# Four-K-tile groups in the first projection stage, norm vectors requested ahead of the rows of x, and a split wait in the last short chunk

## What is computed

```
def first_block(x, c, w_ada, b_ada, ...):
    c_act = jax.nn.silu(c)
    mod = c_act @ w_ada[l] + b_ada[l]                      # 2048 x 12288 matrix, one row of c
    sh_m, sc_m, gt_m, sh_f, sc_f, gt_f = jnp.split(mod[:, None, :], N_MOD, axis=-1)
    h = rmsnorm(x, pre_mix_norm[l]) * (1.0 + sc_m) + sh_m
    proj = h @ w_in[l]
    ...
    y = jnp.concatenate([o_hg, o_gdn], axis=-1) @ w_out[l]
    x = x + gt_m * rmsnorm(y, post_mix_norm[l])
    h = rmsnorm(x, pre_ffn_norm[l]) * (1.0 + sc_f) + sh_f
    y = jnp.square(jax.nn.relu(h @ w_ff1[l])) @ w_ff2[l]
    ...
def conv_ffn(h, w_up, conv_w, conv_b, w_down):             # last stage of the second block
    val, gate = jnp.split(h @ w_up, 2, axis=-1)
    ...                                                    # causal convolution of gate over 3 rows
    return (jax.nn.silu(g) * val) @ w_down                 # inner width 5504 = 5 * 1024 + 384
```

## Time and profile before

| | |
|---|---|
| time, median of 3 runs | 2954.53 us (2952.36 to 2955.92) |
| profiled execution, its own time | 2954.2 us |
| its span | 2952.1 us |
| PE busy | 2707.8 us, 92% of the span |
| DVE busy | 1814.9 us, 61% |
| ACT busy | 1223.6 us, 41% |
| POOL busy | 60.5 us |
| mean traffic from HBM | 190 GB/s |

### The profile page before, as it was taken

How to read it: one execution, slowest core, us unless ns; L and a number is a source line. 1 busy time by engine, 2 the same in 40 slices (tenths; PEclk the granted TensorE clock), 3 DMA queues, 4 the chain that set the end, 5 groups by cost and what they waited for, 6 DMA issues and landing times.

```text
span 2952.1 us, 32514 instructions
## 1 busy us (share of the span) xinstructions
PE 2707.8 (92%) x12554; PEld 2202.9 (75%) x12554; DVE 1814.9 (61%) x2165; ACT 1223.6 (41%) x1558; POOL 60.5 (2%) x84
## 2 busy tenths in 40 slices
PE   4899996798799999999979999998989999999987
PEld 2478885686678888888857777776778888878875
DVE  6678778775775555555664456666455565656455
ACT  2134444433444444444444444443544434344432
POOL 1000000000000000000001000000000000000000
PEclk8899999799999999999989999998999999999998
DMA  9978993054575555555644534534445556465552
GB/s 361 331 216 277 322 333 121 29 200 160 201 285 189 194 185 185 185 185 188 240 154 169 178 127 137 175 125 158 142 159 183 196 173 199 163 201 177 164 163 86
DMA packets 150719, 562.28 MB, mean 190 GB/s; under 512 B 9801, under 2 KB 14024, under 8 KB 146769
## 3 DMA queue, kind: packets, MB, share of 16 engines
q1 hardware_dynamic: 146512, 542.15, 53.8%
q0 software_dynamic: 3920, 18.22, 1.8%
q10 hardware_dynamic: 176, 0.40, 0.0%
HBM read 556.28 MB, written 4.46 MB: 190 GB/s over the span
## 4 chain that ended last, share of the span: by engine, by line
PE 51%; issue 32%; DVE 10%; ACT 3%; DMA 3%; POOL 1%; SPq 0%; DVEq 0%; POOLq 0%; ACTq 0%
PE banks L406 15%; PE banks L408 14%; PE banks L407 14%; PE banks L712 2%; DMA raw_weights<-in_w_ada 2%; DVE weights_low L364 2%; ACT weights_high L351 2%; PE banks L474 1%; DVE mod_in L797 1%; DVE proj L1100 1%; DMA hid_rows<-in_pre_ffn_norm 1%; DVE proj L994 1%; DVE modulation L382 1%; DVE proj L978 1%; PE banks L1136 0%
## 5 line engine op out<-in xcount | busy, mean ns | idle before, releaser
L364 DVE TENSOR_TENSOR weights_low<-raw_weights,weights_high 128x1024 fp32r<-128x1024 f32 (+2 forms) x846 | 990.1, 1179 | 908.8 <-ACT weights_high L351 890.0
L351 ACT ACTIVATE weights_high<-raw_weights 128x1024 fp32r<-128x1024 f32 (+2 forms) x846 | 858.1, 1021 | 1018.4 <-PE banks L408 951.0
L406 PE MATMUL banks<-weights_high,lhs_high 128*128 128x512 f32 (+1 forms) x2208 | 880.4, 399 | 28.2 <-DVE weights_low L364 20.2
L408 PE MATMUL banks<-weights_high,lhs_low 128*128 128x512 f32 (+1 forms) x2208 | 862.8, 391 | 0.0
L407 PE MATMUL banks<-weights_low,lhs_high 128*128 128x512 f32 (+1 forms) x2208 | 861.9, 390 | 0.0
L406 PEld LDWEIGHTS banks<-weights_high,lhs_high 128*128 128x128 f32 x2208 | 418.4, 189 | 122.1 <-DVE weights_low L364 21.9
L408 PEld LDWEIGHTS banks<-weights_high,lhs_low 128*128 128x128 f32 x2208 | 417.5, 189 | 85.9
L407 PEld LDWEIGHTS banks<-weights_low,lhs_high 128*128 128x128 f32 x2208 | 418.9, 190 | 80.6 <-issue 1.0
L406 PE MATMUL banks<-weights_high,hid_high 128*128 128x512 f32 x856 | 337.9, 395 | 20.0 <-DVE hid_low L2448 9.8
L408 PE MATMUL banks<-weights_high,hid_low 128*128 128x512 f32 x856 | 335.5, 392 | 0.0
L407 PE MATMUL banks<-weights_low,hid_high 128*128 128x512 f32 x856 | 335.4, 392 | 0.0
(11 more groups left out here) (404 smaller groups left out, 2082.3 us busy)
## 6 DMA issues: line engine op xcount, KB each, us to landing
raw_weights<-in_w_ff SPq DMA_DIRECT2D x128, 1024.0 KB, 5.0
raw_weights<-in_w_in SPq DMA_DIRECT2D x96, 1024.0 KB, 5.4
raw_weights<-in_w_up SPq DMA_DIRECT2D x80, 1024.0 KB, 4.9
raw_weights<-in_w_ada SPq DMA_DIRECT2D x72, 1024.0 KB, 5.4
raw_weights<-in_w_down SPq DMA_DIRECT2D x42, 1024.0 KB, 5.0
raw_weights<-in_w_out SPq DMA_DIRECT2D x32, 1024.0 KB, 5.1
raw_weights<-in_w_ada SPq DMA_DIRECT2D x32, 768.0 KB, 9.1
first_weights<-in_w_in SPq DMA_DIRECT2D x16, 768.0 KB, 7.8
```

The lines of the kernel that those rows point to most:

```text
L351: act.activation(WHI[:, u % SPN, 0:c.width], RAW[:, n % RAWN, k % 2, 0:c.width], ACT.Copy).then_inc(S("high_made"), 1)
L364: dve.tensor_tensor(WLO[:, u % SPN, 0:c.width], RAW[:, n % RAWN, k % 2, 0:c.width], WHI[:, u % SPN, 0:c.width].bitcast(F32), ALU.subtract) ...
L406: nc.tensor.matmul(o, x, hi, start=(k == 0), stop=False)
L408: mm = nc.tensor.matmul(o, y, hi, start=False, stop=(k == c.kn - 1))
```

## The change

Three edits.

1. `GROUPS` has four groups of four K-tiles. All 32 loads of `w_ada` are 1024 KB, 4 rows of 512 columns for a partition. `FIRST_AFTER` is written anew: tiles 0 and 1 after loads 5 and 7 of the first group, 2, 3 and 4 in the second group, 5 to 8 in the third, 9 to 15 in the fourth. DVE makes a group's columns after one load of the next group instead of two, and the low parts after the fourth load instead of the sixth; the scaling of x's rows comes after the fourth load. POOL waits for the third `mod_made`.
2. In `pool_norm_ffn1` both vectors are requested ahead of the rows of x.
3. In the last short chunk PE waits for 21 ahead of unit 0 and for 22 ahead of unit 2.

```
-        GROUPS = [(0, 6), (6, 6), (12, 4)]
+        GROUPS = [(0, 4), (4, 4), (8, 4), (12, 4)]
...
-        FIRST_AFTER = {MODS[0][13]: [0], MODS[0][15]: [1], MODS[2][3]: [10], MODS[2][5]: [11, 12], MODS[2][7]: [13, 14, 15]}
-        for k in range(8):
-            FIRST_AFTER[MODS[1][2 * k + 1]] = [k + 2]
+        FIRST_AFTER = {MODS[q][n]: tiles for q, n, *tiles in (
+            (0, 5, 0), (0, 7, 1), (1, 1, 2), (1, 3, 3), (1, 7, 4), (2, 1, 5), (2, 3, 6), (2, 5, 7), (2, 7, 8), (3, 1, 9),
+            (3, 3, 10), (3, 5, 11), (3, 7, 12, 13, 14, 15))}
...
-            pool.wait_ge(S("mod_made"), 2)
+            pool.wait_ge(S("mod_made"), 3)
...
-                if n == 5:
+                if n == 3:
                     for t in range(TT):
                         dve_rstd(dve, "norm_in", t)
...
-                    if n == 1:
+                    if n == 0:
                         mod_cols(q - 1)
-                    if n == 5:
+                    if n == 3:
                         input_low(q - 1)
...
-            mod_cols(2)
-            input_low(2)
+            mod_cols(3)
+            input_low(3)
...
-            pool.dma_start(X[:, :, :], a["x"].rearrange("(t p) d -> p t d", p=128)).then_inc(S("x2_in"), 16)
             pool.dma_start(VEC[:, :], row_vector("post_mix_norm")).then_inc(S("vecs_in"), 16)
             pool.dma_start(VEC2, row_vector("pre_ffn_norm")).then_inc(S("vecs_in"), 16)
+            pool.dma_start(X[:, :, :], a["x"].rearrange("(t p) d -> p t d", p=128)).then_inc(S("x2_in"), 16)
...
         def pe_hid2_last(pe):
             all_of(0)(pe)
+            pe.wait_ge(S("hid_low2"), 21)
+
+        def pe_hid2_rest(pe):
             pe.wait_ge(S("hid_low2"), 22)
-        hid2_last = dict(pe=[pe_hid2_last], act=[all_of(1)], dve=[all_of(2)])
+        hid2_last = dict(pe=[pe_hid2_last, None, pe_hid2_rest], act=[all_of(1)], dve=[all_of(2)])
```

## The result

The changed kernel takes 2936.51 us in the median of five runs (four lie at 2934.82 to 2936.69; the fifth, at 6976.8 us, over twice as long for a reason that nothing here shows, is left out of the ratio), against 2954.53 us. The ratio is 0.9938 with a 95% interval of 0.9925 to 0.995: 18 us less, where 17.2 were forecast. The profiled execution took 2936.27 us, its span 2934.5 us.

A forecast was written before the change was run, and what follows sets the result against it. PE was taken as the path, so edits pay only where it stands still; DMA traffic sets the first stage until the last `w_ada` load. 6.4 + 7.4 + 3.4 = 17.2 us off gives 2937.3 us, range 2930 to 2945.

The forecast's parts named there:

- First edit, forecast 6.4 us: First stage: last `w_ada` load in at 127.7 us, stage end at 156.7 against 163.15, gain bounded by 1.7 and 12.2.
- may overlap; I take off half of 4.5, 2.2: First stage: POOL's tiny packets hold engines without moving bytes and may overlap, so 2.2 us of their 4.5 is removed.
- the other 4.5 are tiny packets: First stage: POOL's requests held the engines 6.6 us; masks explain 2.1, tiny packets the other 4.5.
- The later `mod_made` for POOL costs nothing: First stage: POOL's later requests are harmless, since masks are copied at the stage's end and would land before 110 us.
- the prediction's own signs of being wrong: First stage: rate from 40 to 128 us not near 390 GB/s, POOL stopping loads over 4.5 us, or PE awaiting a late tile.
- no stretch that lacks POOL's packets is that low: First stage, against the slower rival (chance 0.02): without POOL's packets no stretch falls to 306 GB/s, where all gains vanish.
- Second edit, forecast 7.4 us: Output projection: vectors land by 703.0, removing PE's 5.62 us wait and 1.8 us of lost clock; bounds 5.6 to 7.4.
- The rival of no order in the queue: Output projection: the vectors come no sooner, the second edit gives nothing, total 2944.7 us; chance 0.04.
- Third edit, forecast 3.4 us: Last chunk: PE begins 3.4 us earlier, after some 6.3 us idle instead of 9.76; bounds 1.7 to 4.2.
- The middle of the program, forecast nothing: Between the output projection and the last chunk: the prediction had no term, 0 us of gain.
- The first stage gains next to nothing: First stage: traffic ends no sooner because 512-column rows move slower, 353 GB/s; total 2943.7 us, chance 0.09.
- DMA keeps up and DVE paces the stage: First stage: loads at 408 GB/s, tiny packets free, no gaps; stage ends at 147.6, total 2928.2 us, chance 0.05.

The follow-up runs named there:

- POOL late: The changed kernel with POOL waiting for the fourth `mod_made` instead of the third before requesting masks, narrow weights and small rows: 2927.84 us, ratio 0.9911 against the kernel before.
- The two built on it: Changed kernel with POOL's requests behind the last group: one cuts the last group in two, 2927.48 us; one makes columns ahead of the next group's first load, 2927.23 us.

## Why the prediction was right, and where it was not

**First edit, forecast 6.4 us: the step that failed is a size.** The mechanism held: from 40 us on the stage runs at the rate of the loads (386 to 401 GB/s outside POOL's requests, forecast 387), and the last four K-tiles come behind the last load. That load was late. The failed step is the term behind "may overlap; I take off half of 4.5, 2.2". Charged were 6.6 - 2.2 = 4.4 us. The requests held the engines for 6.1 us with nothing to take off, 2.4 us of bytes requested behind the last load went ahead of its landing besides, and together they cost 8 to 9 (POOL late in the changed kernel). The name was wrong too: "the other 4.5 are tiny packets" does not fit the packet records, in which packets of 4 KB held 2.7 us of the earlier trace rows and all under 512 B held 1.0. The last load came in at 130.2 instead of 127.7, DVE's sums ended at 133.8 instead of 130.8, and four K-tiles took 22.52 us against the 22.2 charged. Without the requests the load was in at 121.3, where the same count gives 128.4 + 1.5 - 6.6 = 123.3: the rest of the count was 2 us too dear, which hid part of the miss. The sums took 1.95 us, not 2.6. Measured gain 3.7 in this profile and 2.3 in two others, 4.2 alone in the medians; all inside the bounds of 1.7 to 12.2. The median can't tell 4.2 from 6.4, since its ratio leaves 3 to 8 us; the late load can, at 130.22, 130.57 and 130.60 in three profiles. The reading of before was right too: there the low rate of 162 GB/s was SP's wait and not POOL's requests, and moving them gained nothing.

"The later `mod_made` for POOL costs nothing" was right as it stands: with the wait at 2 the changed kernel takes as long as with 3. It missed that a wait at 4 was worth 8 us. The profile of before could not show it, since there PE had products in hand while those loads came in.

Two of the prediction's own signs of being wrong came up: the small requests stopped the loads for longer than 4.5 us, and PE waited 5.92 us for a tile, number 11, ahead of the last column sums. The second can have cost little by itself, for behind that tile's products PE still waited 0.92 us for DVE's sums. And "no stretch that lacks POOL's packets is that low" overlooks the last of the earlier trace rows, 139 GB/s, though that one lies behind the loads of the stage.

**Second edit, forecast 7.4 us: right.** 7.6 us in the profile, 6.5 alone in the medians (4 to 10 by its ratio). The vectors landed 4.8 and 7.0 us after their issue, sooner than the 8.8 that two megabytes of x had taken, so L1632 waits for PE alone, and the clock's part came back: 3.59 us for the second L1580 against 5.39. The rival of no order in the queue did not come; the landings are in the order of the requests here too.

**Third edit, forecast 3.4 us: right.** Idle 6.38 us, and PE restarts 3.37 us sooner. The slow stretch, taken as 4 us long, is 4.9, which takes 0.3 back; that lies inside the bounds.

**The middle of the program, forecast nothing: wrong.** Of the 3.3 us, 2.5 came from slow products that are no longer slow, and 0.8 from a shorter wait near 2865. This and the first edit's 2.7 us too many cancel, so that the total of 17.2 was hit this closely was luck. The 3.3 us are seen in profiles alone; no ratio here is narrow enough to show them. The range of 2930 to 2945 held, by the bounds of the first edit.

**The rivals.** None came in full. "The first stage gains next to nothing" is the nearest: traffic did end late, for POOL's requests and not for the 512-column rows, with which the rate held 386 GB/s or more over the 10 us stretches without those requests. "DMA keeps up and DVE paces the stage" at 2928.2 is close to what POOL late gives, 2927.8, but by the other cause: there PE and the last load bind, and DVE waits for loads until the end.

The best kernel measured is the change with POOL's wait at 4: 2927.84 us, 0.9911 of before, 8 us better than the change itself. The two built on it, at 2927.48 and 2927.23, are no different from it.

## What to carry to other kernels

When a change makes an engine hang on the end of a stream, look at everything else that is requested while the stream is full, and try it behind the last load that counts; where it stood before may have been free only because the waiting engine had work in hand. Price small requests by a run with them and one without, not by their bytes. Before splitting a stage further, read the idle time ahead of its last dependence: here it was 1.28 us, and the split brought nothing. And when parts of a forecast are checked, compare the same instructions in both traces all along the program: a total can be right by two errors that cancel.

## What was not expected of the hardware

- 0.38 MB in small requests on POOL's queue cost a full stream of loads 5 to 7 us, while 0.85 MB of masks on the same queue cost 2. The small ones held the engines 4.0 us and let 0.95 MB from behind the last load go ahead of its landing. Over 10 us the DMA share stays at 0.98 to 1.05: the share does not show this loss, only the rate does (294 to 307 GB/s in four profiles instead of 397).
- Behind the same idle time of 2.8 us PE's granted clock was 0.55 over 3 us in one program, 1.00 in another that came there 12 us sooner, and 0.56 in a third that came 22 us sooner, with the same instructions around it. The slow stretch costs 1.6 us.
- The end of the first stage moves by up to 3.4 us between executions of the same code (162.6, 162.9 and 166.0), so a single profile can't tell edits of 2 us there apart.
